# Feed-forward gate and up products: 18 tile pairs as seven half-token block products with weight sums on GpSimd

## The reference, cut to what matters

```
def swiglu(x, w_gate, w_up, w_down):
    return (jax.nn.silu(x @ w_gate) * (x @ w_up)) @ w_down

f = swiglu(rmsnorm(h, g[0]), ffn_gate[i, 0], ffn_up[i, 0], ffn_down[i, 0])
h = h + MACARON * rmsnorm(f, g[1])
```

## Time and profile before

| | |
|---|---|
| three runs | 2932.53 us median (2929.25 to 2933.09) |
| the profiled execution | 2931.2 us span, 1.3 us under that median |
| PE | 97% of the span busy, 17482 matmuls |
| DVE, ACT, POOL | 53%, 39%, 8% busy |
| weight traffic | 84 GB/s in the mean |
| the four gate and up stretches | 22 pairs each, from 808 us on in the first |

### The profile page before, as it was taken

One profiled execution on the slowest core, in us unless ns is written; L12 is line 12 of the kernel. 1 busy time (PEld: TensorE's weight loads), 2 busy tenths in 40 slices (PEclk: granted clock), 3 DMA queues, 4 the chain that ended last, 5 costly groups with the idle time before them and its releaser, 6 DMA issues.

```text
span 2931.2 us, 43063 instructions
## 1 busy us (share of the span) xinstructions
PE 2843.1 (97%) x17482; PEld 2362.7 (81%) x17482; DVE 1556.0 (53%) x2616; ACT 1136.4 (39%) x1885; POOL 238.4 (8%) x266
## 2 busy tenths in 40 slices
PE   6999899899999999999999999999999999999998
PEld 4866798778888888778888888888888788888887
DVE  7744475554454435856644436744436865544346
ACT  4343454243332223556432225523224564422234
POOL 0000065300000000200000000000000201000001
PEclk9999999999999999999999999999999999999998
DMA  6212000032233232301222332222332301323331
GB/s 243 72 64 72 1 10 4 30 100 95 65 109 99 94 108 101 113 27 57 86 94 95 100 108 87 80 95 99 101 106 101 97 30 51 101 94 101 101 94 58
DMA packets 69780, 244.95 MB, mean 84 GB/s; under 512 B 8464, under 2 KB 10640, under 8 KB 68944
## 3 DMA queue, kind: packets, MB, share of 16 engines
q1 hardware_dynamic: 69584, 242.21, 25.0%
HBM read 234.70 MB, written 3.15 MB: 81 GB/s over the span
## 4 chain that ended last, share of the span: by engine, by line
PE 66%; DVE 5%; ACT 1%; issue 1%; POOL 0%; DVEq 0%; ACTq 0%; POOLq 0%
PE pair L247 20%; PE pair L248 19%; PE pair L249 19%; PE pair L2733 2%; PE pair L2762 2%; DVE work_at L344 1%; PE pair L2772 1%; DVE w_lo_at L190 1%; DVE residual L350 1%; DVE h_lo_at L355 1%; DVE rstd_at L542 1%; ACT w_hi_at L182 1%; PE pair L403 0%; PE pair L409 0%; PE pair L560 0%
## 5 line engine op out<-in xcount | busy, mean ns | idle before, releaser
L247 PE MATMUL pair<-h_hi_at,w_hi_at 128*128 128x512 f32 (+1 forms) x2112 | 780.4, 370 | 17.4 <-DVE h_lo_at L355 13.0
L248 PE MATMUL pair<-h_lo_at,w_hi_at 128*128 128x512 f32 (+1 forms) x2112 | 768.2, 364 | 0.0
L249 PE MATMUL pair<-h_hi_at,w_lo_at 128*128 128x512 f32 (+1 forms) x2112 | 768.2, 364 | 0.0
L182 ACT ACTIVATE w_hi_at<-w_raw 128x1024 fp32r<-128x1024 f32 x340 | 358.8, 1057 | 885.0 <-PE pair L249 862.5
L190 DVE TENSOR_TENSOR w_lo_at<-w_raw,w_hi_at 128x1024 fp32r<-128x1024 f32 x340 | 430.1, 1265 | 311.9 <-ACT w_hi_at L182 311.8
L247 PEld LDWEIGHTS pair<-h_hi_at,w_hi_at 128*128 128x128 f32 x2112 | 398.7, 189 | 98.2 <-DVE h_lo_at L355 20.7
L248 PEld LDWEIGHTS pair<-h_lo_at,w_hi_at 128*128 128x128 f32 x2112 | 399.1, 189 | 62.6 <-issue 0.5
L249 PEld LDWEIGHTS pair<-h_hi_at,w_lo_at 128*128 128x128 f32 x2112 | 399.0, 189 | 62.5
L2487 DVE TENSOR_TENSOR work_at<-pair,rstd_at 128x512 f32<-128x512 f32 x176 | 121.2, 691 | 349.9 <-PE pair L249 349.8
L247 PE MATMUL pair<-a_hi_at,w_hi_at 128*128 128x512 f32 (+1 forms) x792 | 290.1, 366 | 0.0
L248 PE MATMUL pair<-a_lo_at,w_hi_at 128*128 128x512 f32 (+1 forms) x792 | 289.4, 365 | 0.0
(11 more groups left out here) (442 smaller groups left out, 3916.1 us busy)
## 6 DMA issues: line engine op xcount, KB each, us to landing
w_raw<-in_weights SPq DMA_DIRECT2D x431, 512.0 KB, 3.5
residual<-in_x SPq DMA_DIRECT2D x1, 2048.0 KB, 11.4
cos_sin_at<-rope_table SPq DMA_DIRECT2D x2, 1024.0 KB, 4.8
by_sin_at<-delta_at SPq DMA_DIRECT2D x32, 64.0 KB, 2.0
by_sin_at<-kd_at SPq DMA_DIRECT2D x32, 64.0 KB, 2.0
out<-residual SPq DMA_DIRECT2D x16, 128.0 KB, 1.7
q_wide<-in_ctx SPq DMA_DIRECT2D x1, 1024.0 KB, 12.2
rope_table<-zb SPq DMA_DIRECT2D x1, 1024.0 KB, 8.0
```

The lines of the kernel that those rows point to most:

```text
L182: eng.activation(self.w_hi[:, g % self.split].rearrange("p k n -> p (k n)"), self.w_raw[:, slot], ACT.Copy).then_inc(self.w_hi_ready, 1)
L247: pe.matmul(out, sh, mh, start=start, stop=False)
L248: pe.matmul(out, sh, ml, start=False, stop=False)
L249: return pe.matmul(out, sl, mh, start=False, stop=stop)
```

## The change

Tiles 0 to 3 (`FAST` = 4) stay. The 18 pairs 4 to 21 are computed by Strassen's scheme in Winograd's form. One pair is read as a 2 x 2 block product: the rows are gate and up, the contraction is cut into two halves of 4 steps (`gate_0`, `gate_1`, `up_0`, `up_1`), and the tokens are cut into two halves of 256. Seven block products, each 4 x 3 = 12 matmuls of 128x256, take the place of the 48 matmuls of 128x512.

- Weights: each pair needs seven "forms" of 128x512. Three are blocks of `w_raw`, four are sums (`under_left`, `under`, `all_but_right`, `all`), which POOL makes with four `tensor_tensor` of 128x512 into three slots of `exit_work` (`pool_sum`). ACT writes the `hi` of each form (`act_form`) and DVE its `lo` (`dve_form`): 1.75 times the elements, in seven instructions of 128x512 instead of two of 128x1024. The ring of four granules becomes eight places for forms.
- Input: seven "moving" blocks of 128x1024 are made once in each sublayer from `normed` (input x gain x `rstd`, 8 new DVE instructions in tile 0). Four of them are sums (two on DVE, two on POOL), and all seven are rounded by ACT (`act_moving`) and split by DVE (`dve_moving`). Four of the seven overwrite `h_hi`, `h_lo` and so wait for tile 3 on PE.
- Results: for each pair one copy from PSUM (ACT) and five additions of 128x256 with one operand in PSUM (DVE, `dve_combine`: u2, u3, c22, c21, c12) take the place of the two `drain` of 128x512. Products P4 and P3 continue sums that P7 and P5 began in their banks (`reopened`), so PE waits for `u3` ahead of P4, for `c22` ahead of P3, and for a copy ahead of P2.
- `w_split`, on which the fetches wait, now rises by two at the end of each pair's forms.

```
+    def pool_sum(self, pool, i, name):
+        n = 4 * i + self.SUM_ORDER.index(name)
+        if n >= 3:
+            before, old = divmod(n - 3, 4)
+            pool.wait_ge(*self.form_lo(self.FORM * before + self.ORDER.index(self.SUM_ORDER[old]) + 1))
+            pool.wait_ge(*self.summed(n - 1))
...
+        pool.tensor_tensor(self.sum_slot(i, name), *parts, ALU.add).then_inc(self.summed.sem, 1)
+
     def pool(self, pool):
+        src = self.moving_source
+        pool.wait_ge(*self.entry.folded(2))
+        self.pool_sum(pool, 0, "under_left")
+        self.pool_sum(pool, 0, "under")
+        pool.wait_ge(*self.normed(KD))
+        pool.tensor_tensor(src("second"), src("high_1"), src("low_1"), ALU.subtract).then_inc(self.mixed_pool.sem, 1)
+        self.pool_sum(pool, 0, "all_but_right")
+        pool.wait_ge(*self.mixed_dve(2))
+        pool.tensor_tensor(src("corner"), src("first_rest"), src("high_0"), ALU.subtract).then_inc(self.mixed_pool.sem, 1)
+        self.pool_sum(pool, 0, "all")
+        for i in range(1, self.PAIRS):
+            for name in self.SUM_ORDER:
+                self.pool_sum(pool, i, name)
         self.exit.pool(pool)
+
+    def pe_pairs(self, pe):
+        kit = self.kit
+        for i in range(self.PAIRS):
+            for j in (self.P7, self.P1, self.P6, self.P5, self.P2, self.P4, self.P3):
+                q, bank = self.FORM * i + j, "zxyvxzv"[j]
...
+                if i == 0:
+                    pe.wait_ge(*self.moving_rested(self.MOVING.index(self.MOVING_OF[j]) + 1))
...
+                if j == self.P2:
+                    pe.wait_ge(*self.first_copied(i + 1))
+                if j == self.P4:
+                    pe.wait_ge(*self.combined_at(i, "u3"))
+                if j == self.P3:
+                    pe.wait_ge(*self.combined_at(i, "c22"))
+                pe.wait_ge(*self.form_lo(q + 1))
+                w_hi, w_lo = self.form_place(q)
+                hi, lo = self.moving_place(self.MOVING_OF[j])
+                for k in range(4):
+                    last = matmul3(pe, self.pair_bank(i, bank), (w_hi[:, k], w_lo[:, k]), (hi[:, k], lo[:, k]),
+                                   k == 0 and j < 4, k == 3, j >= 4)
+                last.then_inc(self.form_used.sem, 1)
...
+    def act_form(self, act, i, j):
+        kit, q, name = self.kit, self.FORM * i + j, self.ORDER[j]
...
+        if q >= 8:
+            act.wait_ge(*self.form_used(q - 7))
...
+    def dve_form(self, dve, i, j):
...
+        dve.wait_ge(*self.form_hi(q + 1))
+        done = dve.tensor_tensor(lo, self.form_source(i, j), hi.bitcast(F32), ALU.subtract)
+        done.then_inc(self.form_lo.sem, 1)
+        if j == self.FORM - 1:
+            dve.wait_ge(*self.form_lo(q + 1))
+            dve.sem_inc(self.kit.w_split, 2)
+
+    def dve_moving(self, dve, name):
+        hi, lo = self.moving_place(name)
+        dve.wait_ge(*self.moving_rounded(self.MOVING.index(name) + 1))
+        dve.scalar_tensor_tensor(lo, self.moving_source(name), -1.0 if name == "first_rest" else 1.0, hi.bitcast(F32), ALU.mult,
+                                 ALU.subtract).then_inc(self.moving_rested.sem, 1)
...
+            if f == 0:
+                for t in range(KD):
+                    dve.scalar_tensor_tensor(kit.normed[:, t], kit.residual[:, t], self.entry.gain(t), kit.rstd[:, :], ALU.mult,
+                                             ALU.mult).then_inc(self.normed.sem, 1)
...
+        for i in range(self.PAIRS):
+            f, last = self.FAST + i, i == self.PAIRS - 1
+            if i:
+                self.dve_combine(dve, i - 1, "c12")
+            self.dve_form(dve, i + 1, 0)
+            if i:
+                multiply(i - 1)
+            self.dve_form(dve, i + 1, 1)
+            rest(f - 1)
+            self.dve_form(dve, i + 1, 2)
+            self.dve_combine(dve, i, "u2")
+            self.dve_combine(dve, i, "u3")
+            self.dve_form(dve, i + 1, 3)
...
+            self.dve_combine(dve, i, "c22")
+            self.dve_form(dve, i + 1, 4)
...
+            self.dve_form(dve, i + 1, 5)
+            self.dve_combine(dve, i, "c21")
+            self.dve_form(dve, i + 1, 6)
```

More of the change, by code:

```diff
@@ new lines, in form_place, with granule_free, raw @@
+    def form_place(self, q):
+        at = (2 * (self.gf % 4) + q) % 8
+        return [x[:, at // 2, 4 * (at % 2):4 * (at % 2) + 4] for x in (self.kit.w_hi, self.kit.w_lo)]
+    def granule_free(self, j):
+        return max(q for q in range(self.FORM * self.PAIRS) if q % 8 // 2 == (2 * self.PAIRS + j) % 4) + 1
+    def raw(self, i, block):
+        which, part = {"gate_0": (0, 0), "gate_1": (0, 1), "up_0": (1, 0), "up_1": (1, 1)}[block]
+        return self.kit.w_raw[:, (self.gf + 2 * i + which) % RAW, part * 512:part * 512 + 512]
@@ new lines, in landed, with sum_slot, form_source, moving_place @@
+    def landed(self, i, block):
+        g = self.gf + 2 * i + (block[0] == "u")
+        slot = g % RAW
+        return self.kit.w_landed[slot], (g - slot) * (16 // RAW) + 16
+    def sum_slot(self, i, name):
+        return self.kit.exit_work[:, (4 * i + self.SUM_ORDER.index(name)) % 3]
+    def form_source(self, i, j):
+        name = self.ORDER[j]
+        return self.sum_slot(i, name) if name in self.SUM_ORDER else self.raw(i, name)
+    def moving_place(self, name):
+        kit = self.kit
+        h = lambda rows, half: [x[:, rows:rows + 4, cols(half)] for x in kit.h]
+        tail = lambda: [x[:, FT - 2:FT].rearrange("p a (b n) -> p (a b) n", b=2) for x in kit.a]
+        return {"low_0": lambda: h(0, 0), "corner": lambda: h(0, 1), "high_0": lambda: h(4, 0), "high_1": lambda: h(4, 1),
+                "second": tail, "across": lambda: [kit.mixed_in_delta[:, x] for x in (0, 1)],
+                "first_rest": lambda: [kit.mixed_in_delta[:, x] for x in (2, 3)]}[name]()
@@ L2394, in sp, with moving_source @@
+    def moving_source(self, name):
+        kit = self.kit
+        block = lambda rows, half: kit.normed[:, rows:rows + 4, cols(half)]
+        return {"low_0": lambda: block(0, 0), "low_1": lambda: block(0, 1), "high_0": lambda: block(4, 0),
+                "high_1": lambda: block(4, 1), "across": lambda: kit.mixed[:, 0], "first_rest": lambda: kit.mixed[:, 1],
+                "second": lambda: kit.mixed[:, 2], "corner": lambda: kit.mixed[:, 3]}[name]()
     def sp(self, sp):
         fetch_ahead(self.kit, sp, self.g0, self.GRANULES)
-    def pool(self, pool):
-        self.exit.pool(pool)
+    def pool_sum(self, pool, i, name):
[4 more added lines that the diff above has]
+            pool.wait_ge(*self.summed(n - 1))
+        if name == "under_left":
+            for block in ("gate_0", "up_0"):
+                pool.wait_ge(*self.landed(i, block))
+            parts = self.raw(i, "gate_0"), self.raw(i, "up_0")
+        elif name == "under":
+            parts = self.raw(i, "up_0"), self.raw(i, "up_1")
+        elif name == "all_but_right":
+            pool.wait_ge(*self.summed(4 * i + 2))
+            parts = self.sum_slot(i, "under"), self.raw(i, "gate_0")
+        else:
+            pool.wait_ge(*self.summed(4 * i + 3))
+            parts = self.sum_slot(i, "all_but_right"), self.raw(i, "gate_1")
+        pool.tensor_tensor(self.sum_slot(i, name), *parts, ALU.add).then_inc(self.summed.sem, 1)
```

201 lines of the change are left out of this document (185 added, 16 removed).

## The result

The changed kernel takes 3031.93 us (median; 3031.67 to 3032.59), the kernel before 2932.81 us beside it: ratio 1.033, 95% interval 1.0312 to 1.0349, so 3.3% slower. 3034 was predicted, with 2985 to 3072 as the range. The profiled execution has a span of 3030.8 us, 99.6 more than before.

The account below looks back on a forecast made before the run. PE bound the kernel before; DVE, held by POOL's sums, was to bound the pairs. Start 17.2, pairs 7.1 and clock 1 make 25.3 us in each of four sublayers, 101.2; 2931.2 + 101.2 + 1.3 = 3034 us, range 2985 to 3072.

Parts of the forecast that it names:

- The gain on PE: Gate and up pairs: 84 narrow matmuls at 0.120 us take 10.08 us against 10.88, 0.80 us less a pair.
- Weight loads: Rival, PE in the pairs: loads of 0.19 us bound the narrow products, +360 us in all; chance 0.02.
- The pace with GpSimd's sums: Pairs: DVE's 7.3 us, 3.9 held by POOL's sums and 0.1 of ACT waits make 11.3 us a pair.
- The mean over all splits of forms: DVE's form splits (line 2705): 0.69 us alone, but a mean near 1.0 to 1.1 us.
- The step that was mis-sized: Pairs after the first: +0.42 us for each of 17 pairs, +7.1 us a sublayer.
- The start: Stage start: DVE's queue makes `low_0` ready at 847.3, first pair ends at 860.1 instead of 842.9, +17.2 us a sublayer.
- the shape of the wait: Stage start: PE waits 10 us or more before the second product of the first pair.
- The clock: PE after its longer standstills: part of the work at 1.2 GHz, 1 us added a sublayer.
- The rival in which it falls in every pair: PE's clock drops to 1.2 GHz in each pair's wait, +0.5 to +1.5 us on the pace, 3080 to 3140; chance 0.06.
- The turning point: Pairs and start: the change's sign turns at a hold of about 0.8 us a sum.
- DVE just keeps up: Rival: sums fall where DVE reads PSUM or waits, pace 10.5 to 10.8, total 2965 to 2996; chance 0.12.
- Faster: Rival: POOL's sums do not hold DVE, pace is PE's 10.08, total 2900 (2875 to 2915); chance 0.08.

Follow-up runs that it names:

- e1: Changed kernel with each of the four GpSimd weight sums of a pair replaced by three memsets of the same slot: 2920.55 us, 0.9953 of the kernel before.
- e4: Changed kernel with all weight sums and GpSimd's two mixed blocks moved to DVE: 2935.79 us, 1.0006 of the kernel before.
- e6: Changed kernel with FAST 6 instead of 4 and all sums and mixed blocks on DVE: 2911.04 us, 0.9912 of the kernel before.
- e2: Changed kernel with only the sum `under` of each pair replaced by memsets on GpSimd: 2956.27 us, 1.008 of the kernel before.
- e5: Changed kernel with FAST 6 instead of 4, sums still on GpSimd: 2981.13 us, 1.016 of the kernel before.
- e7: e6 with DVE's split of `low_0` moved ahead of its last reading of the last old tile: 2909.71 us, 0.9907 of the kernel before.

## Why the prediction was right

**The gain on PE** was 0.80 us a pair, as reckoned from the earlier trace rows: e1, e4 and e6 run at 10.06 to 10.08, which is 84 x 0.120. The Trainium skill (TensorE: Matmul & The Clock Gate, Back-to-back issue gap) has N/2.4 + 2.5 ns, and says that this is the gap of isolated matmuls; an estimate from it would be 9.2 us a pair, and no run comes near that. Weight loads, at 0.19 us each, did not bound the narrow products.

**The pace with GpSimd's sums** was predicted at 11.3 and is 11.40. Both parts hold: 3.96 us held (3.9 predicted) and 7.44 left for DVE's own work and waits (7.3 + 0.1). Where the two relieved turns lie was only half right: `all_but_right` does meet `c12`, but `under_left` and `under` run one after the other beside two splits and cost nearly their full turns, while the chained sum at 876.35 costs 1.11 and not 1.15. The stall was named at P4's wait for `u3`, 1.2 us; it is there, 1.1 as idle time and 1.3 by the starts. The mean over all splits of forms was named at 1.0 to 1.1 us and is 1.18 (594.1 us for 504): the prediction's own 3.9 us over seven forms would have given more than it wrote down.

**The step that was mis-sized** is the last pair. I took +0.42 for 17 pairs, +7.1; the runs show +0.52 for 16 of them and then a last pair at PE's own speed, since DVE has no next pair's forms and sums to make: 16 x 0.52 - 0.8 = +7.5 on PE's side. It came out close because two small errors point opposite ways, and that is luck.

**The start.** `low_0` was predicted for 847.3 and is ready at 848.19 (its split starts at 846.97 and takes 1.22), or 846.9 when the 1.27 us by which this execution began later are taken off. Its two parts can be checked apart. In e1 the timeline has `low_0` and the two mixed blocks that GpSimd still makes, each of which holds one DVE instruction:

```profile
821.97 3.86 POOL L2497 TENSOR_TENSOR mixed_at<-normed_at 128x1024 f32<-128x1024 f32 x1
824.08 2.83 DVE L191 TENSOR_TENSOR w_lo_at<-w_raw,w_hi_at 128x1024 fp32r<-128x1024 f32 x1
829.99 2.41 POOL L2500 TENSOR_TENSOR mixed_at<-mixed_at,normed_at 128x1024 f32<-128x1024 f32 x1 [2.52 <-DVE mixed_at L2799]
830.43 2.52 DVE L2744 TENSOR_TENSOR a_lo_at<-work_at,a_hi_at 128x512 fp32r<-128x512 f32 x1
843.79 1.22 DVE L2719 SCALAR_TENSOR_TENSOR h_lo_at<-normed_at,h_hi_at 128x1024 fp32r<-128x1024 f32 x1
```

e1's `low_0` is ready at 845.01, 841.7 on the clock of the kernel before (its first reading is 3.32 later), and without the 1.61 and 1.84 us of these two holds at 838.2. The sum had 812.5 + 25.5 = 838.0 for DVE's own work; the holds are then 8.7, where it had 9.3. The end of the first pair was right to a microsecond too, in its own measure, to within 0.3 us between PE's next start and DVE's reading: PE begins the second pair's first product at 860.8, 859.5 on the clock of before, against 860.1.

```profile
L248 PE MATMUL pair<-a_hi_at,w_hi_at x4: 283/283/283, 860.8 to 861.9; 128*128 128x256 f32 x4
```

What was wrong is the shape of the wait. I expected one of 10 us or more before the second product; it is 7.50, because PE had already lost 4.25 us at the weight split of the last old tiles (the row at 826.61), for which the prediction had only "somewhat after it".

**The clock** had a term of 1 us a sublayer. The granted clock is 0.87 over the start and 1.00 in the pairs; behind the wait of 7.50 us the first products start 0.21 us apart in place of 0.12. The rival in which it falls in every pair is refuted: 1.06 us of standing still in each 11.40 leaves it at its upper level of 2.4 GHz. The products that ran at the lower one lie in the start, whose end is set by DVE, so no microsecond of it shows on its own: 16.6 (start, on PE's side) and 7.5 (pairs) already make the 24.1 a sublayer.

**The turning point.** The prediction put it at a hold of 0.8 us a sum. e1 (no hold in the pairs) is faster than before by 0.5% and e2 (three holds) slower by 0.8%, so the sign does lie between no hold and three; the runs changed the number of holds and not their length, and 0.8 itself is not shown.

**The rivals.** "DVE just keeps up" needed a pace of 10.5 to 10.8; it took one hold fewer (e2) or a shorter start (e5) to come near its times. "Faster" needed GpSimd's reads to be harmless, and e1 shows what that would have been worth, 111 us under the changed kernel.

## What to carry to other kernels

Before work is given to GpSimd because it is idle, price it in DVE's time, not in GpSimd's: an addition of 128x512 cost DVE 0.60 us when it made it itself and 0.99 us when GpSimd did. The saving on PE was real wherever DVE let it run (10.06 to 10.08 us a pair in e1, e4, e6 and e7, against 10.88), and what decided was the engine with the second highest load and where the start's extra work could hide: with the sums on DVE and two more tiles ahead of it the same scheme is 0.9% faster than the kernel before. In the profile the sign of such a hold is one engine's instructions of one shape with two lengths and no idle time ahead of them.

## What was not expected of the hardware

A GpSimd memset of 128x512 f32 takes 0.526 us and lengthens DVE's two-operand instructions by 0.01 us at most: 0.689 and 0.691 in the mean beside memsets, 0.683 in e4 with GpSimd still. The Trainium skill (SBUF — State Buffer, Who interferes with whom) says that such a DVE instruction contends with a GpSimd instruction that reads SBUF and not with one that only writes it; e1 agrees with both halves of that.

The hold works on GpSimd too: in e1 its addition of 128x1024 took 3.86 us when it began at 821.97, with DVE already in a two-operand instruction, and 2.41 the second time. The 1.45 us more reach past the end of that DVE instruction (822.42) to about the end of the next one (823.56), which also has two operands in SBUF. So the turns do not always alternate one by one, as the prediction had it: here DVE had two in a row.
